# Twelve gates of the last unit computed early, and the output weights converted inside the attention stage

## The reference, cut to what matters

```python
h = rmsnorm(x, pre_norm)
proj = h @ w_in                       # queries, keys, values of four groups, and the gate (width 2048)
y = concatenate([diff_attention, stick_breaking, forgetting_attention, memory_attention])  # width 2048
y = y * silu(gate)
out = x + rmsnorm(y @ w_out, post_norm)
```

## Time and profile before

| | |
|---|---|
| three runs | 2808.32, 2809.97, 2815.78 us; median 2809.97 |
| the profiled execution | 2811.71 us, its span 2809.9 us |
| TensorE busy | 2476.0 us, 88% of the span |
| VectorE, ScalarE, GpSimd busy | 1834.0, 1639.6, 1078.2 us |
| attention ends (start of the output stage) | 2433.4 us |
| tile 2 of the output stage starts | 2506.5 us |

### The profile page before, as it was taken

How to read it: one execution, slowest core, us unless ns; L and a number is a source line. 1 busy time by engine, 2 the same in 40 slices (tenths; PEclk the granted TensorE clock), 3 DMA queues, 4 the chain that set the end, 5 groups by cost and what they waited for, 6 DMA issues and landing times. The chain is left out here.

```text
span 2809.9 us, 72476 instructions
## 1 busy us (share of the span) xinstructions
PE 2476.0 (88%) x27130; PEld 1670.0 (59%) x27130; DVE 1834.0 (65%) x5100; ACT 1639.6 (58%) x4435; POOL 1078.2 (38%) x1718
## 2 busy tenths in 40 slices
PE   3678999998998999998999999989999997589998
PEld 2355666666576666665766666667666665334443
DVE  5553898876558988675699887656998765321111
ACT  4333786557757865577588555866875567422122
POOL 0010345545624545555245455652555555300000
PEclk9989999999999999999999999999999998699999
DMA  3243687449957864599587646984874368762431
GB/s 109 60 114 77 117 151 128 93 87 150 168 107 133 148 120 89 99 163 170 110 143 130 117 84 119 156 168 96 158 139 104 63 120 150 158 187 75 120 105 45
DMA packets 935544, 339.34 MB, mean 121 GB/s; under 512 B 767724, under 2 KB 926324, under 8 KB 935180
## 3 DMA queue, kind: packets, MB, share of 16 engines
q1 hardware_dynamic: 934744, 333.66, 60.3%
q0 software_dynamic: 448, 1.05, 0.1%
HBM read 79.66 MB, written 26.84 MB: 38 GB/s over the span
## 5 line engine op out<-in xcount | busy, mean ns | idle before, releaser
L1343 POOL TENSOR_TENSOR rows<-rows 128x512 f16<-128x512 f32 (+3 forms) x864 | 866.9, 1017 | 931.5 <-ACT rows L1301 928.1
L1147 PE MATMUL job<-wt,big 128*128 128x128 f16 x10752 | 682.4, 221 | 48.4 <-DVE gate_s L1433 17.8
L1147 PEld LDWEIGHTS job<-wt,big 128*128 128x128 f16 x10752 | 631.1, 99 | 116.9 <-DVE gate_s L1433 29.6
L1147 PE MATMUL job<-big,wt 128*128 128x512 f16 x2688 | 674.6, 383 | 11.0 <-PEq L660 4.6
L1301 ACT CAST rows<-rows 128x512 f16<-128x512 f32 (+3 forms) x864 | 462.8, 548 | 225.2 <-DVE rows L1425 115.8
L1208 PE MATMUL mixed<-values,rows 128*128 128x64 f16 (+1 forms) x8544 | 444.3, 201 | 97.1 <-DMA rows<-rows 63.8
L1208 PEld LDWEIGHTS mixed<-values,rows 128*128 128x128 f16 x8544 | 389.1, 99 | 228.5 <-DMA rows<-rows 97.2
L1313 ACT ACTIVATE rows<-rows,neg_max 128x512 f32<-128x512 f32 (+3 forms) x704 | 447.7, 638 | 74.7 <-DVE neg_max L1400 72.3
L1392 DVE TENSOR_SCALAR_CACHE_REDUCE rows<-scores 128x512 f32<-128x512 f32 (+3 forms) x704 | 399.8, 588 | 124.0 <-POOL rows L1343 92.0
L1193 PE MATMUL scores<-stack 128*128 128x512 f16 (+3 forms) x1600 | 432.1, 349 | 27.1 <-DVE rows L1392 18.3
L1147 PEld LDWEIGHTS job<-big,wt 128*128 128x128 f16 x2688 | 243.6, 99 | 250.0 <-issue 14.5
(11 more groups left out here) (136 smaller groups left out, 2524.7 us busy)
## 6 DMA issues: line engine op xcount, KB each, us to landing
stack<-planes SPq DMA_DIRECT2D x160, 192.0 KB
ws<-w_in SPq DMA_DIRECT2D x56, 512.0 KB, 4.6
y_halves<-y_out_halves SPq DMA_DIRECT2D x64, 256.0 KB, 2.7
rows<-y_halves SPq DMA_DIRECT2D x16, 1024.0 KB, 8.1
rows<-rows SPq DMA_TRANSPOSE x864, 3.3
rows<-x SPq DMA_DIRECT2D x16, 512.0 KB, 3.6
ws<-w_out SPq DMA_DIRECT2D x16, 512.0 KB, 3.8
stack<-x SPq DMA_DIRECT2D x16, 512.0 KB, 5.5
```

The costliest lines, as they stand in the source:

```text
L1147: last = nc.tensor.matmul(dst, lhs, rhs, start=(k0 == 0 and q == 0), stop=(k1 == KT and q == len(pairs) - 1))
L1343: nc.gpsimd.tensor_tensor(halves_of(tau, 1, w), scored(plan.chunk_at(g, m, k0), 0, w), halves_of(tau, 0, w), ALU.subtract).then_inc(low_po ...
```

## The change

It does five things.

- The gates of the last unit's steps 244 to 255 (`late`) become a queue of their own. They no longer wait for the end of step g - 2 but for the last load of the unit's `stack` quarters, since their 12 results go into the first two `planes`, which are free from then on. The order of TensorE's ranks stays gate, y, mix, score, project; "late" stands between score and project.
- When all gates and projections have been computed (`LAST_READ`), the 16 strips of `w_out` are loaded, converted to `wo` (over `hT`) and widened inside the attention stage, by the same queues as the strips of `w_in`; the 2 us of `EASY` are not added for them.
- The first pair of y tiles is loaded in the attention stage too ("early_y", into the memory of `wt`), when its last step is stored and the same condition holds.
- The output stage has no loading and converting of weights left; TensorE takes all 16 tiles by the loop that it had for tiles 2 to 15.
- The ranks and `AHEAD` and `LATE` have new values. TensorE's and ScalarE's rank orders are the same as before, but for "late". VectorE's order was low, weigh, widen, post, near, combine, copy, scan, and is near, low, combine, weigh, widen, post, copy, scan.

```diff
RANK = {
-    "pe": {"gate": -0.56896, "y": 0.65716, "mix": 2.26812, "score": 3.66995, "project": 6.06207},
-    "act": {"take": -0.56306, "beta": 0.18730, "job": 5.24904, "stick": 7.44050, "convert": 7.47892,
+    "pe": {"gate": -0.56896, "y": -0.54978, "mix": -0.01946, "score": 3.00000, "late": 3.26562, "project": 6.80653},
+    "act": {"take": -0.56306, "beta": 0.18730, "job": 0.79550, "stick": 7.44050, "convert": 7.47892,
             "hi": 7.82832, "exp": 8.61381},
-    "dve": {"low": 3.02114, "weigh": 3.66090, "lo_dve": 5.58491, "widen": 5.68258, "post": 5.97032,
-            "near": 6.20571, "combine": 6.74865, "copy": 7.57977, "scan": 8.13881},
+    "dve": {"lo_dve": -0.17433, "near": 0.67284, "low": 4.36593, "combine": 4.69889, "weigh": 5.59694,
+            "widen": 5.68258, "post": 6.68901, "copy": 7.19439, "scan": 8.92021},
     "pool": {"root": 0.00000, "lo": 1.00000},
     "sp": {"pairs": 0.50000, "turn": 0.80000, "stacks": 0.90000, "strip": 1.00000, "sums": 2.00000,
-            "store": 3.00000, "near_in": 4.00000},
+            "store": 3.00000, "near_in": 4.00000, "early_y": 5.00000},
 }
-AHEAD = {0: 0.10000, 1: 0.51500, 2: 0.58645, 3: 0.72022}
-SLACK, LATE = 3.83945, 5.18846
+AHEAD = {0: 0.10000, 1: 0.51500, 2: 0.58645, 3: 0.68071}
+SLACK, LATE = 3.83945, 7.48359
 DVE_LOW = {"mem": 0, "stick": 0, "diff": 0, "forget": 0}
...
         self.nt = nt = seq // P
+        self.last = len(UNIT) - 1
+        self.late = self.last * nt + 4
         self.k_tiles = k_tiles
...
             q["y"].append((("y", g), ("y", g), [("post", g)], 0.11, PE_LAG))
-            q["gate"].append((None, ("gate", t, G, g), [("w", t, G)] + ([("post", g - 2)] if g >= 2 else []),
-                              0.0, 0.0))
+            if g >= self.late:
+                need = [("w", t, G)] + [("stacks", t, c) for c in range(nt * P // BANK)]
+            else:
+                need = [("w", t, G)] + ([("post", g - 2)] if g >= 2 else [])
+            q["late" if g >= self.late else "gate"].append((None, ("gate", t, G, g), need, 0.0, 0.0))
         chunks = nt * P // BANK
...
             q["widen"].append((("w_lo", n), ("convert", (n, t, kind)), [("w_hi", n)], 1.14, 0.08))
+        for k in range(2 * self.k_tiles):
+            n = len(self.converts) + k
+            q["strip"].append((("strip", n), ("strip", n), [("w_lo", n - 2)], 0.64, 4.0))
+            q["convert"].append((("w_hi", n), ("convert", (n, self.last, k)),
+                                 [("strip", n), ("gate_hi", self.n_steps - 1), ("gate_hi", self.late - 1),
+                                  ("v_hi", self.last, V, nt - 1)], 0.95, 0.1))
+            q["widen"].append((("w_lo", n), ("convert", (n, self.last, k)), [("w_hi", n)], 1.14, 0.08))
+        q["early_y"].append((("early_y",), ("early_y",),
+                             [("store", self.last * nt + 3), ("gate_hi", self.n_steps - 1),
+                              ("gate_hi", self.late - 1),
+                                  ("v_hi", self.last, V, nt - 1)], 1.3, 8.0))
         q["store"] = deque((("store", g), ("store", g), [("y_lo", g)], 0.64, 2.6)
...
                 for name, rank in RANK[e].items():
-                    if name in ("gate", "project", "y") and opened:
+                    if name in ("gate", "late", "project", "y") and opened:
                         continue
...
                         continue
-                    if name in ("gate", "project", "y") and jobs >= J_BANKS:
+                    if name in ("gate", "late", "project", "y") and jobs >= J_BANKS:
                         bank = end.get(("j_free", jobs - J_BANKS))
...
                         at = max(at, bank + HOP)
-                    if name in ("strip", "store"):
+                    if name == "store" or name == "strip" and task[1][1] < len(self.converts):
                         at += EASY
...
                 if e == "pe" and opened:
-                    rank = RANK[e]["gate" if opened[1] == "g" else "project"]
+                    rank = RANK[e]["project" if opened[1] != "g" else "late" if opened[4] >= self.late else "gate"]
                     if pick is None or (free[e], rank) < pick[:2]:
...
             at, _, name, e = best
-            if name in ("gate", "project"):
+            if name in ("gate", "late", "project"):
                 what, t, kind, index = q[name].popleft()[1]
...
         need = [("j_hi", n)]
-        if what == "g" and index >= 2:
+        if what == "g" and 2 <= index < self.late:
             need.append(("post", index - 2))
...
+        LATE_G = plan.late
+        late_gate = planes[:, 0:2, :].rearrange("p a s -> p (a s)").bitcast(F32).rearrange("p (i f) -> p i f", f=P)
+        LAST_READ = max(job[0] for job in plan.job_of.values())
+        def gated(g):
+            return late_gate[:, g - LATE_G] if g >= LATE_G else gate_s[:, g % 2, :]
         def soft_count(n):
...
+        PAIRS = NT // 2
+        yl = [buffer.rearrange("p (h k s) -> p h k s", h=2, k=YT) for buffer in (
+            wt[:, :, :, :, :].rearrange("p a b k n -> p (a b k n)"), rows_flat[:, 0:YT * 2 * P].bitcast(F16))]
+        y_in = [sem(f"y_landed{b}") for b in range(2)]
+        def load_y(sp, q):
+            src = y_dram[:, :, q * 2 * P:(q + 1) * 2 * P].rearrange("h (k f) s -> f h k s", f=P)
+            for h in range(2):
+                sp.dma_start(yl[q % 2][:, h], src[:, h]).then_inc(y_in[q % 2], 16)
         with nc.Block() as block:
...
                 def load_weights(n):
-                    t, kind = plan.converts[n]
                     if n >= 2:
                         sp.wait_ge(w_ready, n - 1)
+                    if n >= len(plan.converts):
+                        sp.dma_start(ws[:, n % 2, :], w_out_rows[n - len(plan.converts)]) \
+                            .then_inc(w_in_sem[n % 2], 16)
+                        return
+                    t, kind = plan.converts[n]
                     at = UNIT[t].col[kind]
...
                         sp.dma_start(near_f[:, :], near_dram[lane]).then_inc(near_landed, 16)
+                    if op == "early_y":
+                        yg = (plan.last * NT + 3) // 4
+                        for b in range(2):
+                            sp.wait_ge(y_stored[b], STORE * ((yg - b) // 2 + 1))
+                        sp.wait_ge(j_full, LAST_READ + 1)
+                        load_y(sp, 0)
                     if op == "sums":
...
                     act.wait_ge(w_in_sem[n % 2], (n // 2 + 1) * 16)
+                    if n >= len(plan.converts):
+                        act.wait_ge(j_full, LAST_READ + 1)
+                        nc.scalar.activation(wo[:, 0, kind], ws[:, n % 2, :], ACT.Copy, scale=W_SCALE) \
+                            .then_inc(w_hi, 1)
+                        return
                     nc.scalar.activation(wt[:, kind, 0],
...
                     dve.wait_ge(w_hi, n + 1)
+                    if n >= len(plan.converts):
+                        nc.vector.scalar_tensor_tensor(wo[:, 1, kind], ws[:, n % 2, :], W_SCALE, wo[:, 0, kind],
+                                                       op0=ALU.mult, op1=ALU.subtract).then_inc(w_ready, 1)
+                        return
                     nc.vector.scalar_tensor_tensor(
...
-                    if g >= 2:
+                    if g >= LATE_G:
+                        for c in range(NC):
+                            dve.wait_ge(stacked[c], STACKED[plan.last])
+                    elif g >= 2:
                         dve.wait_ge(post_step, POST_AT[g - 1])
                     dve.wait_ge(j_hi, plan.gate_job[g][0] + 1)
-                    nc.vector.scalar_tensor_tensor(gate_s[:, g % 2, :], gate_t[:, g % 2, :], 1.0,
+                    nc.vector.scalar_tensor_tensor(gated(g), gate_t[:, g % 2, :], 1.0,
                                                    job_out(plan.gate_job[g])[0], op0=ALU.add, op1=ALU.mult) \
...
                     at = POST_AT[g]
-                    y, gate = y_f[:, g % 2, :], gate_s[:, g % 2, :]
+                    y, gate = y_f[:, g % 2, :], gated(g)
                     if g >= 2:
...
-        PAIRS = NT // 2
-        yl = [rows_flat[:, b * YT * 2 * P:(b + 1) * YT * 2 * P].bitcast(F16)
-              .rearrange("p (h k s) -> p h k s", h=2, k=YT) for b in range(2)]
         flat = stack_flat[:, 0:5 * 2 * D].bitcast(F32)
...
         scrap = [j_bank[0], j_bank[1]]
-        wo_in, y_in, x_in2, out_stored = ([sem(f"{n}{b}") for b in range(2)]
-                                          for n in ("wo_landed", "y_landed", "res_landed", "out_stored"))
-        wo_hi, wo_ready, gain_in, out_full, out_sq, out_root, out_step, out_ready = (
-            sem(n) for n in ("wo_hi", "wo_ready", "gain_landed", "out_full", "out_sq", "out_root", "out_step",
-                             "out_ready"))
+        x_in2, out_stored = ([sem(f"{n}{b}") for b in range(2)] for n in ("res_landed", "out_stored"))
+        gain_in, out_full, out_sq, out_root, out_step, out_ready = (
```

(45 more changed lines are left out.)

## The result

The changed kernel takes 2817.62 us (median of 8 runs, 2812.05 to 2821.74), the kernel before 2809.87 (8 runs). The ratio is 1.0025, 95% interval 1.0014 to 1.0037: slower, by less than the 0.3% named in the prediction, but outside the noise. The forecast was 2799, faster. The profiled execution took 2815.26 us, its span is 2813.5.

The account below looks back on a forecast made before the run. Attention's end was taken as paced by transposes on nearly full DMA engines, and the output stage's start as waiting for weights. 2811.7 - 29.3 (output stage) + 18.4 (strips) = 2800.8, less 1.7 to the median: 2799 us, range 2779 to 2822.

Parts of the forecast that it names:

- 0.3% named in the prediction: Whole kernel: 0.3%, 8.4 us, taken as about the least change that can be told.
- Everything else: Rank orders, AHEAD and other work in three stages: costed at nothing, within 5 us either way.
- The output stage: Stage after attention: 376.5 us now, 347.2 after, 29.3 less, with weights already there and 16 tiles at 20.9 us.
- The term for the clock: Output stage's first matmuls: low granted clock loses 1.0 + 0.7 us, taken as 2.
- The gates: Late gates 244 to 255 in attention: costed at nothing, bounds -7.6 and +7.5 us; all done near 2355.
- The strips: 16 w_out strips loaded and converted in attention's last 70 us: attention ends 18.4 us later, through DMA.
- the DMA sum: Attention's last 70 us: 60.9 + 32 + 7 = 99.9 us of DMA work, at 1.13 88.4 us, 18.4 later.
- It fits, barely: ScalarE in attention's last 70 us: conversions add 16.8 us to 48.6, giving 65.4 of 70.
- transposes queue behind strips: SyncE's DMA queue in attention: a transpose issued behind a strip gets nothing until the strip is through.
- rows named for late landings: Profile rows with DMA shares near 1.1 and transposes landing late, said to agree with ring order as far as they go.
- The "slower" rival: Attention's end: a loop of high half, low half, transpose, landing decides; 16 x 3.05 = 48.8 us, 2829; chance 0.13.
- What the widen adds on GpSimd: Form of the slower rival: GpSimd also loses 1.2 us a strip, 16 x 4.25 = 68 us, 2848; chance 0.04.

Follow-up runs that it names:

- the first experiment: The changed kernel with the ranks, AHEAD, SLACK and LATE of the kernel before; 2792.39 us, ratio 0.9944.
- the loads alone: The changed kernel with old constants, its 16 w_out loads kept but not converted on ScalarE and VectorE; 2795.01 us, a single run.
- neither: The changed kernel with old constants, without the 16 w_out loads, their conversions and all their waits, early y pair kept; 2778.78 us, a single run.

## Why the prediction was wrong

**The step that failed** is "Everything else": the ranks, AHEAD and LATE, costed at nothing within 5 us. They cost 14.5 us by the end of unit 14. Alone in the kernel before they cost 13.8 us, and undone in the changed kernel they give back 25.2, to 2792.4: the change without them is faster. The argument was that TensorE is busy 9 tenths in those units and its work is the same. That bounds nothing: a tenth of 2000 us is 200 us of waiting, and an order in which VectorE serves another task first moves some of it. TensorE's busy time did not grow (2473.2 us for 2476.0); what grew is the waiting between. The step also took the rank order, which for TensorE is unchanged, for the order of the instructions, which follows from all engines' tasks: VectorE's new ranks alone change TensorE's list too. It misread the ranks as well: VectorE's combine now also passes weigh, while weigh and low stand as before. AHEAD was read as 2.5 us moved between units; in unit 6 it cost 5.5 us. That these waits are the ones on the row maximum is not shown. The range (2779 to 2822) held the time by luck: it reached that far for DMA work that doesn't fit and for strips that hold up the ring, and not for the constants. So the sign came out wrong.

**The output stage** was right: 347.2 us forecast, 345.1 measured. The term for the clock was counted twice. The granted clock was 0.50 in the first 4 us of matmuls and 0.72 in the next 2, and the first two tiles took 43.96 us from start to start where later pairs took 41.44, so 2.5 us were lost. But the 20.9 us a tile already held such a start: in the kernel before tile 2 began behind a gap at a clock of 0.50 and took 23.0 us, and those after it 20.72 each. With 20.72 the sum is 16 x 20.72 + 2.5 = 334.0, and 334.2 were measured.

**The gates** were right with the old constants: the last job started at 2349.6, for "near 2355", in the first experiment. In the changed kernel it started at 2376.1, 74.9 us into the last unit for 66.8; its timeline, against the earlier trace rows:

```profile
2376.07 0.83 PE L1192 MATMUL job<-wt,big 128*128 128x128 f16 x12
2377.53 0.83 PE L1192 MATMUL job<-wt,big 128*128 128x128 f16 x12
```

Its matmuls come in two halves of 12 with other work between. So the strips started later and had less attention left to hide under; that this is why the last unit cost 20.4 for 16.9 is likely, but not shown.

**The strips** came out near the right size, for half of the reason. 18.4 us were forecast from the DMA sum; 16.9 (old constants) and 20.4 measured, at a share of 1.06 (1.13 taken). But leaving the loads out brings 1.7 us back, and the sum says 18. ScalarE's conversions, listed as "It fits, barely", are a bound of the same size. The throughput sum left out that in a ring without slack each delay of a buffer counts, also where the engine has time to spare on average. That transposes queue behind strips was right: all 34 landed after the strip ahead of them. The rows named for late landings hold none beside a strip, but the trace has them: 4.2 us in the median from 2018 to 2026 in the kernel before, for 3.3 over all. The "slower" rival had the mechanism of the ring, with 3.05 us a strip; measured, both causes together cost (158.2 - 146.2) / 16 = 0.75 us a strip. They overlap (the table above), and gaps take up the rest. What the widen adds on GpSimd is small in all: low halves average 1185 ns in the 68 us with conversions and 1064 without, and 0.12 us times 32 low halves is 4 us of GpSimd's work. By single low halves it is plain: in the first experiment's 68 us the seven that overlap a widen took 1.6 to 2.1 us, and none of the others more than 1.16. The Trainium skill has a lock between the two for such pairs of operations ("SBUF — State Buffer", SBUF: two separate sides); the traces agree in direction.

## What to carry to other kernels

A table of scheduling constants that comes with a structural change is a change of its own: undo it alone before anything is said of the structure. When two resources are both nearly full under added work, removing either load shows nothing, and only the run without both, or with less of the work, tells what the work costs. Move only as much under a full stage as the next stage can't hide: here eight strips of sixteen, with tile 0 ahead of tile 1 in the output stage, made the fastest kernel. And look for what stands behind a moved load: the y load behind the last transpose delayed the last store by 2.2 us.

## What was unexpected of the hardware

- A transpose queued behind the early y pair (2 MB) took 5.69 us to issue on SyncE, where the median is 1.28, and landed 9.3 us after the issue began. Landing times don't show what this does to the transposes behind it in SyncE's list: with the loads alone a transpose was issued 1.86 us after its low half on average (the 40 chunks of the table), with neither 0.93.
- A transpose takes nearly the same time to issue at any width: in the kernel before 1.20 us at 128x256 and 1.27 at 128x1024 (medians), while the landing goes from 2.3 to 3.3 us.
- On nearly full DMA engines 16 loads (8.4 MB) could be added at a cost of 1.7 us (158.2 for 156.5, one profile each), as long as ScalarE held the ring up as well.
